# Strassen products for feature pairs in all three feed-forward blocks, with three of the four weight sums made by adding transfers

## The reference, cut to what matters

```python
def conv_ffn(x, ln_g, up_w, conv_w, conv_b, down_w):          # blocks 0 and 1
    u = causal_dwconv(rms_norm(x, ln_g) @ up_w, conv_w, conv_b)   # 3 taps along the positions
    gate, up = u[..., :FFN_DIM], u[..., FFN_DIM:]
    return (jax.nn.silu(gate) * up) @ down_w

def swiglu(xn, w_gate, w_up, w_down):                         # block 2
    return (jax.nn.silu(xn @ w_gate) * (xn @ w_up)) @ w_down
```

## Time and profile before

| | us |
|---|---|
| median of three runs | 2397.32 (2397.05 to 2397.42) |
| the profiled execution, its own time | 2399.27 |
| its span, first to last instruction | 2397.5 |
| granted TensorE clock, mean | 0.998 |

### The profile page before, as it was taken

How to read it: one execution, slowest core, us unless ns; L and a number is a source line. 1 busy time by engine, 2 the same in 40 slices (tenths; PEclk the granted TensorE clock), 3 DMA queues, 4 the chain that set the end, 5 groups by cost and what they waited for, 6 DMA issues and landing times.

```text
span 2397.5 us, 30764 instructions
## 1 busy us (share of the span) xinstructions
PE 2371.2 (99%) x11952; PEld 1944.2 (81%) x11952; DVE 1484.8 (62%) x2356; ACT 1086.1 (45%) x1878; POOL 357.9 (15%) x286
## 2 busy tenths in 40 slices
PE   8999999999999999999999999999999999999999
PEld 6677878888888877788888877787788878898987
DVE  6778776763666777766456547534655445873763
ACT  6654554442445677644234334324443334442433
POOL 0252252210111000122011100001210001100001
PEclk9999999999999999999999999999999999999999
DMA  4532223223223221232332332231234332233232
GB/s 164 109 93 79 80 70 99 97 86 108 97 83 120 75 76 49 73 108 92 93 106 87 91 131 84 71 102 57 72 123 136 115 106 79 81 105 99 95 97 89
DMA packets 74847, 226.24 MB, mean 94 GB/s; under 512 B 8144, under 2 KB 12368, under 8 KB 74576
## 3 DMA queue, kind: packets, MB, share of 16 engines
q1 hardware_dynamic: 70272, 215.90, 28.1%
q10 hardware_dynamic: 4432, 8.39, 2.0%
HBM read 215.87 MB, written 8.39 MB: 94 GB/s over the span
## 4 chain that ended last, share of the span: by engine, by line
PE 60%; DVE 1%; ACT 0%; issue 0%; DMA 0%; POOL 0%; POOLq 0%; DVEq 0%; ACTq 0%; SPq 0%
PE bank L1272 59%; PE bank L1276 1%; DVE t L2230 1%; DVE t L2233 1%; ACT t L1715 0%; DVE t L2241 0%; DMA t<-in_w 0%; POOL t L2877 0%; ACT t L1718 0%; ACT L1718 0%; DVE t L2237 0%; DVE t L2798 0%; POOLq L3100 0%; DVEq L3100 0%; DVE t L2644 0%
## 5 line engine op out<-in xcount | busy, mean ns | idle before, releaser
L1272 PE MATMUL bank<-t 128*128 128x512 f32 (+5 forms) x11526 | 2346.4, 369 | 19.1 <-DVE t L2233 7.9
L1272 PEld LDWEIGHTS bank<-t 128*128 128x128 f32 (+2 forms) x11526 | 1901.0, 186 | 433.3 <-issue 80.1
L1715 ACT ACTIVATE t<-t 128x1024 fp32r<-128x1024 f32 (+5 forms) x676 | 564.0, 847 | 564.6 <-PE bank L1272 276.6
L2230 DVE TENSOR_TENSOR t<-t 128x1024 fp32r<-128x1024 f32 (+7 forms) x774 | 687.3, 901 | 202.9 <-ACT t L1715 192.4
L1718 ACT ACTIVATE t<-t 128x512 f32<-128x512 f32 (+6 forms) x610 | 367.5, 616 | 455.8 <-DVE t L2230 307.1
L2877 POOL TENSOR_TENSOR t<-t 128x512 f32<-128x512 f32 (+4 forms) x206 | 316.3, 1542 | 1551.9 <-ACT t L1718 559.7
L2230 DVE TENSOR_TENSOR t<-bank,t 128x512 f32<-128x512 f32 (+4 forms) x434 | 279.2, 648 | 425.2 <-PE bank L1272 414.7
L2233 DVE SCALAR_TENSOR_TENSOR t<-t 128x512 f32<-128x512 f32 (+5 forms) x536 | 386.6, 733 | 102.3 <-ACT t L1718 63.8
L1715 ACT ACTIVATE t<-bank 128x512 f32<-128x512 f32 (+4 forms) x184 | 84.7, 477 | 205.4 <-PE bank L1276 146.9
L2880 POOL TENSOR_SCALAR t<-t 128x128 f32<-128x128 f32 (+3 forms) x64 | 40.9, 645 | 478.6 <-ACT t L1715 247.6
L2233 DVE SCALAR_TENSOR_TENSOR t<-bank,t 128x512 f32<-128x512 f32 x56 | 38.5, 688 | 68.8 <-PE bank L1272 68.8
(11 more groups left out here) (30 smaller groups left out, 53.0 us busy)
## 6 DMA issues: line engine op xcount, KB each, us to landing
t<-in_w SPq DMA_DIRECT2D x304, 512.0 KB, 3.4
t<-in_w SPq DMA_DIRECT2D x48, 384.0 KB, 3.0
t<-in_w SPq DMA_DIRECT2D x56, 320.0 KB, 3.0
t<-in_w SPq DMA_DIRECT2D x28, 256.0 KB, 2.8
tab<-t ACTq DMA_DIRECT2D x1, 2560.0 KB
t<-in_x SPq DMA_DIRECT2D x8, 256.0 KB, 5.0
t<-tab SPq DMA_DIRECT2D x8, 256.0 KB, 3.7
spill<-t ACTq DMA_DIRECT2D x1, 2048.0 KB, 8.3
```

Source lines behind the costliest of these rows:

```text
L1272: return eng.matmul(out, lhs, rhs, start=start, stop=stop, skip_group_check=loose)
L1715: return eng.activation(out, in_, ACT.Copy, scale=scale)
L2230: return eng.tensor_tensor(out, a, b, o)
```

## The change

It makes Strassen pairs in all three blocks: 6 tiles f in block 0, the same 6 in block 1, and 10 (before 11) in block 2. In blocks 0 and 1 the two taps, the multiplication and the rest of such a pair are all on DVE, and the activations' sums are made there too.

The weight sums change hands. A pair's four half units now lie side by side in memory, P numbers each: gate top, up top, up bottom, gate bottom. SP loads the first three (`base`, 768 KB) into a buffer; POOL issues a transfer that adds the last two of memory onto its first two halves (`add1`, 512 KB, accumulate), and one that adds the buffer's first half onto its last (`add2`, 256 KB). DVE makes the fourth sum alone (`add3`, 512 columns). They are planned 19, 15, 9 and 3 ticks ahead of t. There are two such buffers (three in block 2). s12 is one unit, 1024 columns in one piece; s34 comes from two buffers, so that ACT and DVE take two instructions of 512 columns each for its split and its cut, and signal once.

The order of products is now p1 p5 p6 p3 p7 p2 p4. So s12 is wanted at t + 1 and s34 at t + 3. The splits of both stay where the unit's place puts them; their cuts are moved to one tick behind the split (before: two).

```diff
-QUADS = (4, 5, 7, 8, 10, 12, 13, 15, 16, 18, 19)
-PRODUCTS = ("p1", "p2", "p6", "p5", "p7", "p3", "p4")
+QUADS = {0: (9, 12, 14, 16, 18, 20), 1: (9, 12, 14, 16, 18, 20), 2: (4, 7, 8, 10, 12, 13, 15, 16, 18, 19)}
+SUM_AGES = ((19, 15, 9, 3),) * 3
+PRODUCTS = ("p1", "p5", "p6", "p3", "p7", "p2", "p4")
+QUAD_HALF = {"p1": (0, 0), "p5": (1, 0), "p6": (1, 1), "p7": (2, 0), "p3": (2, 1), "p4": (3, 0), "p2": (3, 1)}
...
+        sources = (("raw", first, S), ("s12", (s, f), UNIT), ("s34", (s, f), UNIT), ("raw", last, UNIT))
         for i, product in enumerate(PRODUCTS):
...
+            if QUAD_HALF[product][0] == len(g.units):
+                g.units.append(self.ring(sources[len(g.units)]))
+            self.put(Piece(g, QUAD_HALF[product][0], i, i + 1, i == 0))
...
+        for u in g.units[1:3]:
+            self.cut_at = {at: [v for v in units if v != u] for at, units in self.cut_at.items()}
+            self.cut_at.setdefault(next(at for at, units in self.split_at.items() if u in units) + 1, []).append(u)
+        for name, age in zip(("base", "add1", "add2", "add3"), SUM_AGES[s]):
+            self.start(name, (s, f), t - age)
...
     def split(u):
-        n = plan.units[u][3]
-        w.wait_ge(*K.source_ready(u))
+        for ready in K.source_ready(u):
+            w.wait_ge(*ready)
         if u >= N_W:
             w.wait_ge(*K.unit_done(u - N_W))
-        copy(buf.his[u % N_W][:, 0:n], K.source(u)).then_inc(*sig["cut_hi"].up(u))
+        for a, b, of in K.source(u):
+            t = copy(buf.his[u % N_W][:, a:b], of)
+        t.then_inc(*sig["cut_hi"].up(u))
...
     def cut(u):
-        n = plan.units[u][3]
         w.wait_ge(*sig["cut_hi"].at(u))
-        tt(buf.los[u % N_W][:, 0:n], K.source(u), buf.his[u % N_W][:, 0:n].bitcast(F), SUB).then_inc(*sig["cut"].up(u))
+        for a, b, of in K.source(u):
+            t = tt(buf.los[u % N_W][:, a:b], of, buf.his[u % N_W][:, a:b].bitcast(F), SUB)
+        t.then_inc(*sig["cut"].up(u))
...
+            tt(buf.sum4[:, :], K.sums(sf)[:, 2 * S:3 * S], buf.raws[last % N_W][:, S:UNIT], ADD).then_inc(*sig["sum"].up(sf))
...
+            w.wait_ge(*K.based(sf))
+            eng.dma_start(K.sums(sf)[:, 0:UNIT], K.region(region)[:, S:3 * S], accum_op=ADD).then_inc(
+                *sig.added[i][0].up())
...
+            w.wait_ge(*K.added(sf, 0))
+            eng.dma_start(K.sums(sf)[:, 2 * S:3 * S], K.sums(sf)[:, 0:S], accum_op=ADD).then_inc(*sig.added[i][1].up())
```

More of the change, by code:

```diff
@@ L312, in quad @@
-        self.quad_units[f] = (r, *g.units)
-        for u, end in zip(g.units, (("bank", (*key, "a")), ("product", (f, "p5")), ("bank", (*key, "d")),
+        region = self.region((gate, 0, 4, gate_c + f * P, P), (up, 0, 4, up_c + f * P, P),
+                             (up, 4, 4, up_c + f * P, P), (gate, 4, 4, gate_c + f * P, P))
+        first = self.load(region, 0, S)
+        last = self.load(region, 2 * S, UNIT)
+        g = Group(key, False, FFN_IN[s], 0, [], DC, 0, P, H2)
+        sources = (("raw", first, S), ("s12", (s, f), UNIT), ("s34", (s, f), UNIT), ("raw", last, UNIT))
@@ L877, in __init__ @@
         self.tb2 = [Dma(sem(f"tb2{i}")) for i in range(4)]
+        self.base = [Dma(sem(f"base{i}")) for i in range(3)]
+        self.added = [[Dma(sem(f"added{i}{j}")) for j in range(2)] for i in range(3)]
         self.spill, self.mem, self.out = (Dma(sem(n)) for n in ("spill", "mem", "out"))
@@ L967, in ffn @@
         self.fv = [sb(st, [P, S]) for _ in range(6)]
[L968 to L969 removed]
+        self.fu_all = sb(st, [P, 3 * (S + 4)])
+        self.fu = [self.fu_all[:, i * (S + 4):(i + 1) * (S + 4)] for i in range(3)]
+        own = sb(st, [P, 3 * S])
+        self.sums = [[own, self.scratch], [own, self.scratch], [own, self.scratch, self.fu_all]]
+        self.sum4 = sb(st, [P, S])
     def diff(self, st):
@@ L3007, in gpsimd_program @@
         ssm(T)
+        adds(T)
         ffn(T)
@@ L3026, in load, with base @@
                 w.wait_ge(*done)
-        eng.dma_start(buf.raws[r % N_W][:, 0:n], dram["w"][off:off + P * n].rearrange("(p n) -> p n", p=P)).then_inc(
-            *sig.w[r % N_W].up())
+        eng.dma_start(buf.raws[r % N_W][:, 0:n], K.region(region)[:, at_:at_ + n]).then_inc(*sig.w[r % N_W].up())
+    def base(sf):
+        region, *_ = plan.quad_units[sf]
+        i, turn, before = K.sums_at(sf)
+        if before:
+            w.wait_ge(*sig["cut"].at(plan.quad_units[before][4]))
+        elif i == 1:
+            for j in range(4):
+                w.wait_ge(*sig["tee_lo"].at((sf[0], 3), j))
+        else:
+            w.wait_ge(*sig["lo"].at(*h_of(sf[0], 0)))
+        if turn > 1:
+            w.wait_ge(*sig.base[i].at(turn - 1))
+        eng.dma_start(K.sums(sf)[:, 0:3 * S], K.region(region)[:, 0:3 * S]).then_inc(*sig.base[i].up())
     for c in range(DC):
@@ L3042, in sync_program @@
                 load(plan.units[u][1] + N_W)
+        for sf in at("base", T):
+            base(sf)
         for h in at("tb", T):
```

427 lines of the change are left out of this document (254 added, 173 removed).

## The result

The changed kernel takes 2436.01 us, the median of four runs (2435.01 to 2437.67), against 2397.37 (2397.05 to 2399.64) for the kernel before on the same chip: a ratio of 1.016, 95% interval 1.0146 to 1.0174. It is slower by 39 us. The prediction was 2426, in a range of 2387 to 2445, with 0.78 on slower.

What follows compares the result with a forecast made beforehand. PE, busy 99% of the span, was taken as the bound. From the profiled 2399.3 us, - 7.7 - 1.7 + 6.5 + 0.7 + 31 gave 2428.1, as a median 2426, in a range of 2387 to 2445.

Steps and rivals of the forecast that it cites:

- case A: Whole kernel: the sum of all predicted terms, first- and second-order waits included, gives 2426 us; chance 45%.
- What PE saves: All blocks: twelve pairs become Strassen at 0.70 us each, one in block 2 goes back at 0.67; -7.7 us.
- Before's wait of 1.7 us: Block 2, second pair: PE's wait for sums DVE cut late goes, as the sums are made elsewhere; -1.7 us.
- Blocks 0 and 1: Waits at f = 9 and, with DVE falling behind, from f = 14 on: 15.5 us per block, +31.
- my chain: Blocks 0 and 1, from plain pair's start n: up evacuated n + 14.6, cuts n + 18.1, wanted n + 15.2; wait 2.85.
- rival B: Blocks 0 and 1: only first-order waits, DVE does not fall behind as turns with ACT overlap better; 2403 us, chance 20%.
- The second stop: Blocks 0 and 1, start of the plain pair after a Strassen one: PE waits 0.8 us, 0.1 with POOL at 1.5.
- Block 2: s34's cut late: 1.3 us at five pairs after a plain one, +6.5, and 0.1 at others, +0.7; 7.2 together.
- the step that cost the transfers at nothing: Base and adding transfers: some 17 us of room for both adding ones, taken as under 12, so hidden at no cost.
- rival D: Adding transfers slower than 17 us together, 1.6 us late at each of 22 pairs; 2461 us or more, chance 17%.
- The small ones: Waits of 0.1 us where nothing waits for POOL, +0.7; activations' sums in blocks 0 and 1 nought, 0 to 3 in range.
- Rival C: s34's cut is in time, needing 1.3 us less in block 2's chain, so the kernel is faster; 2388 us, chance 18%.

Runs made afterwards that it cites:

- the kernel with all four edits: Changed kernel with s34's split a tick earlier, rounding in blocks 0 and 1 a tick later, products ahead of Strassen pairs on DVE, block 2's transfers earlier: 2386.85 us.
- the one with block 2 alone: Changed kernel with Strassen pairs in block 2 only, the same 10, and plain pairs in blocks 0 and 1: 2414.53 us, ratio 1.007.
- The early split: Changed kernel with the split of s34 one tick earlier on ACT, ahead of p1's copy, the rounding and tap 0: 2415.31 us, ratio 1.0071.
- the late rounding: Changed kernel with the rounding of a Strassen pair's product in blocks 0 and 1 one tick later on ACT, its rest one later on DVE: 2428.12 us.

## Why the prediction was right, and by how much it was off

**The forecast held: case A, 39 us slower, 29 predicted.** With the kernel without stops at 2383.5 of span, the changed one has 50.3 more: 35.0 of idle PE, about 0.25 for each of 33 stops until PE's row of matmuls is full again (24.42 us for a period, less 2.68 idle, is 21.74, where 10.91 + 10.07 = 20.98 would do: 0.76 for three stops), so 8.3, 4.0 of lower clock in block 2, and 1.7 of it at 1430 us, where the kernel without stops has no such fall: 49.0. What is left, 1.3, is within what two runs differ by. One sign of the prediction did not come: PE's busy time was to fall by about 8, and refilling and clock raised it by 3.7.

**What PE saves: 8.4 predicted for twelve pairs, 9.1 measured** (2395.93 against 2386.85). In the trace a plain pair is 10.91 and a Strassen one 10.07, which would make 10.1.

**Before's wait of 1.7 us** The earlier trace rows is gone. It stood at the second pair, f = 5, which is a plain one now, and nothing at all stops in block 2 of the kernel with all four edits.

**Blocks 0 and 1: 31 predicted.** The changed kernel less the one with block 2 alone is 21.5, and with the 9.1 they save 30.6. The mechanism is the one in the prediction: the evacuation of up begins 2.6 us after up ended (some 3.1 in my chain, whose n + 14.6 is its end), s34's cuts behind it. That the sum came out within 0.4 us is in part luck. I had no term for what a stop costs beyond its idle time. The stops themselves are 24.2 us and not 31: the first wait, 2.85 in my chain, is 1.38 at p3 and 0.61 at p6, which I had not named. The refilling, 28 x 0.25 = 7.0, made up the difference. Per period my chain had 3.65 and it is 24.42 - 20.98 = 3.44. The early split gives the tick back and gains 21; the late rounding takes ACT's first wait out; with both, no stop over 0.53 us is left there. So rival B, that the orders would overlap better, is refuted, and its argument (DVE's work fits in the period) was true all the same: it fits once the orders are changed.

**The second stop: 0.8 predicted, 0.69 + 0.25 measured.** It hangs on POOL's 2.20 us: with DVE's product in its place it went. The Strassen pair's own rounding has no part in it.

**Block 2: 7.2 predicted, 18.6 measured** (2414.53 less 2395.93, of which 1.7 is the clock's fall at 1410 us, outside the block). This is the one term that was clearly mis-sized. The first stop was 1.16 for 1.3, since POOL took 1.30 there and not 1.52. The error is the step that cost the transfers at nothing: "their queue is POOL's, whose multiplications behind them begin after the landing in most places". The median length was as I took it, 5.5 and 4.0, 9.5 together for "under 12", and the pair's own sums came nearly in time. But the 17 us of room are the room of a pair's own sums; the product of the plain pair before it stands in POOL's queue behind the transfers of the pair after it, and for those the plan leaves less. SP issued f = 19's base transfer at 2306.39, 21.7 us before f = 19 would have begun, in place of some 27 (4 ticks of 1.44, 8 of a plain pair, 10.91, and 7 of f = 18, 10.07). It and the first adding transfer then took 7.2 and 7.6 us to land, the longest of block 2, where the medians there are 5.1 and 5.7. So the mechanism is rival D's in part, "rounding waits for POOL", by some 5 us of late beginning and 4 of slow landing at f = 18. In block 2 it cost 5.8 us of idle and 4.0 of clock; with those transfers planned some ticks earlier it costs nothing, and the medians show 9.3.

**The small ones.** 0.1 us at each pair after a Strassen one or a down projection, 0.7 in all, showed nowhere. The activations' sums cost nothing: the kernel with all four edits makes them and has no stop. Rival C, faster, needed 1.3 us less in the chain; the early split and DVE's product are just such cuts. Its condition was not met; its price, 9.4 below before, is near the 11.8 by which the kernel with all four edits beats its own group's runs before.

**The two rules.** POOL's product took 2.20 us beside DVE and 1.30 where DVE stood idle, so the trace agrees with the rule of the Trainium skill, "SBUF — State Buffer", "Who interferes with whom", that a DVE instruction with two SBUF inputs contends with a GpSimd instruction that reads SBUF. The estimate by the Trainium skill, "DMA: Bandwidth & Descriptors", "Anatomy of one DMA", 3.2 and 2.6 us for the two adding transfers, was too low: 5.5 and 4.0. It would have told no more than my own bounds: with all four edits the 256 KB ones take 5.2 in the median and cost nothing.

## What to carry to other kernels

Fewer matmuls are worth what they save only if the hand-overs around them keep their distance: here some 9 us of saved work brought 50 us of stops and of what follows them, and moving two instructions in ACT's order by one tick, the products ahead of Strassen pairs to another engine and three transfers by a few ticks brought the whole gain out. When a unit is wanted a tick earlier, move its producer in its engine's queue by a tick as well, and look for what stands ahead of it that waits for a third engine. A lead that a plan counts in ticks is not a lead in time: read in the trace when the transfer was issued, and when it landed. Keep work that others wait for out of a queue that waits for transfers, and look there for the transfers of the next user too, not only for one's own.

## What the runs showed of the hardware

- The granted clock fell to 0.50 at the end of the stop of 1.94 us and within the stop of 4.72 us, and cost 1.7 and 2.3 us of work done at the lower level. It did not fall after a stop of 1.97 us at f = 15, nor after the many shorter ones in blocks 0 and 1. In the other kernels of this case it fell after stops of 2.03, 2.42 and 2.91 us and not after others of 2.06, 2.26 and 2.77, and in four kernels it fell between 1407 and 1430 us where PE did not stop: the length of the stop alone doesn't decide. After 440 us each fall cost at most 1.7 us, but the one around the stop of 4.72 us, which went on for twice as long.
- A stop of PE costs about 0.25 us more than its idle time, which its busy time hides: PE's busy time was 3.7 us above before's, though the kernel with the same matmuls and no such stop has 11.7 less than before's.
- An adding transfer of 512 KB took 5.5 us (a plain one 3.5 in the same kernel), one of 256 KB 4.0 (medians; up to 7.6 and 8.0), and each issue held POOL for 0.87 us.
- Where DVE stood idle POOL's product of 512 columns took 1.30 us, beside DVE's work 2.20.
